# Two-layer decoder trunk in fp32: where transposes stand among matmuls, a diagonal level in 64-key parts, and the order of two row requests

## The reference

```
h    = rms_norm(x);  proj = h @ w_in               # q, f, i, gate of a gated recurrence, q, k, v of attention
y_hg = chunked_gated_recurrence(...)               # 4 heads of 128, decay from a cumulative sum
y_at = dilated_attention(...)                      # 8 heads of 64, three patterns merged
x    = x + concat(y_hg, y_at) @ w_out
q    = rms_norm(x) @ wq;  k, v = split(rms_norm(mem) @ wkv)     # 4 heads of 256, 256 memory tokens
x    = x + softmax(q k^T / 16) v @ wo
x    = x + moe(rms_norm(x))                        # 4 groups of 4 experts of width 512; best group, best 2 in it
```

## Time and profile before

| what | value |
|---|---|
| median of 3 runs | 1014.53 us (1013.32 to 1015.21) |
| profiled execution, its own time | 1015.3 us |
| its span, first to last instruction | 1013.4 us |
| TensorE busy | 988.4 us, 98% of the span |
| VectorE, ScalarE, GpSimd busy | 485.1, 136.5, 98.4 us |
| chain that ended last, by engine | PE 94%, DMA 2%, DVE 2%, POOL 1%, issue 1% |
| DMA, slices of 25.3 us from 811 to 988 us | 403, 421, 420, 420, 421, 420, 417 GB/s |
| mean granted TensorE clock | 0.993 of full speed |

### The profile page before, as it was taken

The page is one execution under the profiler, slowest core; times in us unless marked ns, Lnnn a source line. Parts: engine busy times, 40 slices in busy tenths (PEclk is TensorE's granted clock), DMA queues, the critical chain, the costliest instruction groups (busy, mean ns, idle before and its releaser), DMA issues.

```text
span 1013.4 us, 11694 instructions
## 1 busy us (share of the span) xinstructions
PE 988.4 (98%) x4744; PEld 532.2 (53%) x4744; DVE 485.1 (48%) x845; ACT 136.5 (13%) x323; POOL 98.4 (10%) x123
## 2 busy tenths in 40 slices
PE   8999999999998999999999999999999899999996
PEld 7658445669574453333333854465974333333332
DVE  2534386766554224422444636776656434444334
ACT  3211001412011010101112000041020101111111
POOL 3051032000020000000000513210000100000000
PEclk9999999999999999999999999999999999999999
DMA  9973101864289999999999420077385899999995
GB/s 356 425 310 122 45 1 48 372 249 163 88 309 377 397 424 419 420 423 420 421 422 420 180 84 1 1 288 284 133 316 210 340 403 421 420 420 421 420 417 200
DMA packets 44828, 293.61 MB, mean 290 GB/s; under 512 B 5472, under 2 KB 5728, under 8 KB 13024
## 3 DMA queue, kind: packets, MB, share of 16 engines
q1 hardware_dynamic: 38000, 266.36, 64.9%
q10 hardware_dynamic: 5616, 22.24, 5.6%
q0 software_dynamic: 1152, 4.19, 1.1%
HBM read 283.33 MB, written 9.44 MB: 289 GB/s over the span
## 4 chain that ended last, share of the span: by engine, by line
PE 94%; DMA 2%; DVE 2%; POOL 1%; issue 1%; ACT 0%; POOLq 0%; DVEq 0%; ACTq 0%
PE bank L1040 20%; PE bank L1110 11%; PE bank L598 8%; PE bank L1071 6%; PE bank L628 6%; PE bank L813 6%; PE bank L630 5%; PE bank L608 5%; PE bank L867 5%; PE bank L931 5%; PE bank L701 5%; PE bank L588 2%; DMA rot<-by_slot 2%; PE bank L901 1%; PE bank L885 1%; PE bank L1064 1%
## 5 line engine op out<-in xcount | busy, mean ns | idle before, releaser
L1040 PE MATMUL bank<-ring,hT 128*64 128x512 f32 x704 | 195.0, 593 | 0.0
L1040 PEld LDWEIGHTS bank<-ring,hT 128*64 128x64 f32 x704 | 62.3, 137 | 87.4 <-issue 87.4
L598 PE MATMUL bank<-ring,hT 128*128 128x512 f32 x192 | 85.6, 599 | 0.0
L1993 DVE TENSOR_TENSOR x<-bank,x 128x512 f32<-128x512 f32 x64 | 44.3, 692 | 51.1 <-PE bank L1071 51.1
L2011 DVE TENSOR_SCALAR xs<-xs 128x512 f32<-128x512 f32 x8 | 3.4, 427 | 124.2 <-ACT xs L1347 124.1
L1071 PE MATMUL bank<-PT 128*128 128x512 f32 x128 | 59.2, 605 | 0.0
L1110 PE MATMUL bank<-ring,Vx 128*64 128x512 f32 x160 | 57.9, 603 | 0.0
L598 PEld LDWEIGHTS bank<-ring,hT 128*128 128x128 f32 x192 | 35.5, 190 | 40.7 <-issue 40.2
L1110 PE MATMUL bank<-ring,xs 128*64 128x512 f32 x224 | 56.7, 595 | 0.0
L608 PE MATMUL bank<-hT,ring 128*128 128x256 f32 x256 | 55.7, 379 | 0.8 <-DVE hT L1622 0.8
L813 PE MATMUL bank<-ring,hT 128*128 128x512 f32 x128 | 56.3, 595 | 0.1
(11 more groups left out here) (302 smaller groups left out, 1550.0 us busy)
## 6 DMA issues: line engine op xcount, KB each, us to landing
ring<-in_w_experts SPq DMA_DIRECT2D x146, 1024.0 KB, 14.0
ring<-in_w_mix SPq DMA_DIRECT2D x60, 1024.0 KB, 14.1
work<-in_w_experts SPq DMA_DIRECT2D x20, 1024.0 KB, 11.2
late<-in_w_experts SPq DMA_DIRECT2D x10, 1024.0 KB, 13.2
late<-in_w_mix ACTq DMA_DIRECT2D x4, 2048.0 KB, 10.2
keys<-in_w_experts SPq DMA_DIRECT2D x8, 1024.0 KB, 16.4
rot<-by_slot ACTq DMA_DIRECT2D x14, 512.0 KB, 8.0
by_slot<-late ACTq DMA_DIRECT2D x1, 4096.0 KB, 37.9
```

Of the source, the lines that this page charges most:

```text
L598: last = nc.tensor.matmul(b[:, :], lhs[:, c, m * P:(m + 1) * P], w[:, c, :], start=(c == 0), stop=(c == C - 1))
L1040: last = nc.tensor.matmul(banks[2 + g][b2 * CAP:(b2 + 1) * CAP, :], rows_T_of(p)[:, c, b2 * CAP:(b2 + 1) * CAP], w, start=(c == 0), stop=( ...
L1993: V.tensor_tensor(xv, banks[OUT_BANK[n][m]][:, :], xv, ALU.add).then_inc(r_added[L], 1)
```

## The change

Four edits. (1) In both layers the transposes pt00 and pt01 go ahead of the scores sx11, on TensorE and in the order of banks; the vector engine's two copies go ahead of its maximum of sx11. By the bank plan sx11, pt00 and pt01 exchange the banks 4, 5 and 6. (2) In the first layer the eighth key-value job is cut: chunks 0 to 4, t1_00, t1_01, chunk 5, t1_10, chunks 6 and 7, t1_11. The second layer's order is as it was. (3) Level 0 is made in two 64-key parts like the levels above it, with 64 streamed, and copied in two parts. (4) In step p = 0 of the routed experts ScalarE waits for the scatter and requests the rows of pair 1 right after the first half of the gate unit, ahead of the read of the whole gate unit and of the exponential; the rows of pair 2 are requested after the exponential as before.

```diff
-             ("q_4", "A"), ("sx10", "A"), ("sx11", "A")]
-    jobs += [(f"pt0{jb}", "D") for jb in range(2)] + [("px0", "D"), ("px1", "A")]
+             ("q_4", "A"), ("sx10", "A")]
+    jobs += [(f"pt0{jb}", "D") for jb in range(2)] + [("sx11", "A"), ("px0", "D"), ("px1", "A")]
...
-                    for j in range(8):
+                    for j in range(7):
...
                     if L:
                         kv_job(7, banks[0], kv_unit, memT, chunks)
+                    else:
+                        kv_job(7, banks[7], unit("v1"), hT, chunks)
...
                         transposes(L, f"t1_{m}{c2}", by_columns(xs, m, c2))
-                    last_values(range(5, 6) if m == 0 else range(6, C))
+                        if (m, c2) == (0, 1):
+                            last_values(range(5, 6))
+                        elif (m, c2) == (1, 1 if L else 0):
+                            last_values(range(6, C))
...
-                                if j:
-                                    last = nc.tensor.matmul(b[HALF * i:HALF * (i + 1), a * QUARTER:(a + 1) * QUARTER], K[:, a, m * P + HALF * i:m * P + HALF * (i + 1)],
-                                                            later(Q[:, a, m * P + HALF * i:m * P + HALF * (i + 1)], j), start=True, stop=True)
-                            if j == 0:
-                                last = nc.tensor.matmul(b[:, a * P:(a + 1) * P], K[:, a, m * P:(m + 1) * P],
-                                                        Q[:, a, m * P:(m + 1) * P], start=True, stop=True)
+                                own = slice(m * P + HALF * i, m * P + HALF * (i + 1))
+                                n = QUARTER if j else HALF
+                                last = nc.tensor.matmul(b[HALF * i:HALF * (i + 1), a * n:(a + 1) * n], K[:, a, own],
+                                                        later(Q[:, a, own], j) if j else Q[:, a, own], start=True, stop=True)
...
                 memory_scores(1, 0, "q_2")
+                memory_weights(0)
                 memory_scores(1, 1, "q_4")
-                memory_weights(0)
...
                     if p == 0:
                         units_read(p, "half")
+                        act.wait_ge(r_sent[L], 16 * 2 * M)
+                        load_rows(1)
                     units_read(p, "gate")
-                    if p == 0:
-                        act.wait_ge(r_sent[L], 16 * 2 * M)
                     nc.scalar.activation(rexp_of[L], banks[2][:, :], ACT.Exp, scale=-1.0).then_inc(r_gexp[L], 1)
                     if p == 0:
-                        for q in (1, 2):
-                            load_rows(q)
+                        load_rows(2)
...
-                            emptied(V.copy_predicated(S[:, m, :, :], lev[:, j, :].bitcast(I32).unsqueeze(1).to_broadcast([P, HG_HEADS, P]),
-                                                      found[:, :].rearrange("p (a t) -> p a t", t=P)))
+                            for i in range(2):
+                                own = slice(HALF * i, HALF * (i + 1))
+                                copied = V.copy_predicated(S[own, m, :, own], lev[own, 0, own].bitcast(I32).unsqueeze(1).to_broadcast([HALF, HG_HEADS, HALF]),
+                                                           found[own, 0:HG_HEADS * HALF].rearrange("p (a t) -> p a t", t=HALF))
+                            emptied(copied)
...
                 memory_max(1, 0)
+                memory_kept(0)
                 memory_max(1, 1)
-                memory_kept(0)
```

## The result

| | before | after |
|---|---|---|
| median | 1014.08 us, 4 runs (1013.32 to 1015.21) | 1004.91 us, 4 runs (1003.76 to 1005.29) |
| profiled execution, span | 1015.3, 1013.4 us | 1003.76, 1001.8 us |
| TensorE busy | 988.4 us | 982.9 us |

The ratio of the runs is 0.9903, 95% interval 0.9888 to 0.9919: 9.8 us less, between 8.2 and 11.4 (the two medians alone differ by 9.2). A second series on another chip gave 1005.25 us (4 runs) and 0.9891 (0.9876 to 0.9906). The forecast was 1006.9, its range 1005.2 to 1009.6: the sign was right and the gain larger than forecast. Lines of the kernel after are 2 to 6 higher than before: L1064 became L1067, L1089 L1092, L1110 L1113, L1040 L1043, L885 L888, L901 L904, L701 L706, L739 and L736 both L742. "Landing" is the time from a DMA request to the arrival of its data.

The account below looks back on a forecast made before the run. TensorE, busy nearly the whole span, was taken as the bound. Terms 2.60 + 0.77 + 1.26 + 2.55 + 0.40 = 7.58 us off the profiled 1015.3 gave 1007.7, or 1006.9 against the median; range 1005.2 to 1009.6.

Parts of the forecast that it names:

- second layer's rows: Second layer's row stage: the earlier request lets rows land up to 0.8 us earlier with effect; gain taken 0.40 us.
- first layer's rows: First layer's row stage: request near 310.6, rows land before TensorE needs them, so the whole wait goes; gain 2.55 us.
- diagonal level: Level 0 in 64-key parts: 1.15 us instead of 1.78, 0.63 per layer, 1.26 us in all.
- Shares' transposes: Memory stage: the wait before the values goes, 1.30 us per layer, 2.60 us in all.
- rival (b): Memory stage: last shares come so late that their transposes wait, taking back 2.60 us: 1009.5 us; chance 0.08.
- Tokens: First layer's last key-value job: token transposes placed inside it remove the next projection's wait; gain 0.77 us.
- rival (e): Diagonal level takes 1.95 us, nothing of a piece hidden; 1.6 us back, 1008.5 us; chance 0.02.
- rival (a): First layer's row request queues behind the keys' load on ScalarE; 1.42 us of wait stays, 1008.3 us; chance 0.10.
- Rival (d), the clock: Second layer's row stage: half clock lasts on into the matmuls, making the kernel slower, up to 1026.7 us; chance 0.04.
- Rival (c), the weights: Second layer's weights run dry before the last down product; TensorE stalls 2.2 us, 1009.1 us; chance 0.07.

Follow-up runs that it names:

- the fillers: Kernel before plus two idle matmuls in the row stage of both layers, the first only, or the second only: ratios 0.9956, 0.9978, 0.9977.
- after_again: The changed kernel, unaltered, measured again beside a version with the second layer's old order of row requests: 1005.25 us, ratio 0.9891.
- the variants: Changed kernel with two idle matmuls in the second layer's row stage, its exponential ahead of the row request, or both: 1004.94, 1004.73, 1005.31 us.

## Where the prediction was right, and where it was wrong

The change is worth 7.58 us in the prediction's sum and 9.47 in the chains. Of the 1.89 between them 1.54 are in one term, the second layer's rows; 0.53 and 0.22 are the matmuls behind the waits that went, 0.07 the first layer's rows, and the diagonal level (0.24) and the end (0.23) go the other way. The median lies only 0.3 below the range, and the kernel before alone had medians from 1014.08 to 1015.98 on the chips used, but the gain is above the forecast's in both series.

- **Shares' transposes: right, too small.** The wait went and nothing took its place, so rival (b) is out; the spare time before the last transposes was 0.55, for 0.8 in the prediction. The upper bound was the wait, 1.30; measured 1.56 and 1.57. The first matmuls behind a wait had cost 0.27 more than the same ones in a running stream. The same at the tokens, 0.23.
- **Tokens: right**, 0.76 of wait, plus that 0.23.
- **Diagonal level: right.** 1.08 against my 1.15 and the 1.95 of rival (e); 0.19 came back in the job behind it, which I had not in the sum. By the rule of the Trainium skill, TensorE: Matmul & The Clock Gate, section Part 3, the prediction's estimate would have been the 1.95; these records, whose weights use all 128 rows, ran at 34 ns each, so the measurement decides against it. The vector engine's pair of 64x256 copies takes 0.89 to 0.90, the lower end of the 0.9 to 1.5.
- **First layer's rows: right**, 2.62 for 2.55. The wait went wholly, since the request left at 306.6 and took 8.4; rival (a) would have had it land behind 318.1, it was 315.0, with the keys' load in the same queue.
- **Second layer's rows: the step that failed.** "I take a gain of 0.4", with rows that land "up to 0.8 earlier with effect". The term took the 7.87 as fixed within a microsecond and let "fewer weights are ahead of the rows" count for under one microsecond. In fact the earlier 2 MB had been requested 6.8 before, the next stood 0.4 behind, and 7.87 became 4.4. With it the second of TensorE's two idle stretches went (2.30 and 1.14 before, 2.81 after, in the timelines of TensorE). That is 0.63 less idle time for the 0.4 of the sum. The other 1.31 of the 1.94 is the same work done faster, and the sum has no term for it: the clock was low for less long, and the down product of pair 0 alone has 7.10 instead of 8.23. That this hangs on the order is shown by the stage in eleven profiles (24.5 to 24.9 against 25.6 to 27.0); over the runs it is about 1 by the medians, not clear of nothing.
- **Rival (d), the clock: the right place with the wrong sign.** The wait for the activation did grow, to 2.8 for the forecast 2.7, and the clock did fall behind it (798 to 802 had 0.58), but for some 3.4 us (0.42 of 4 us, twice) instead of 6.8 (the earlier trace rows and its neighbours: 0.06, 0.50 and 0.29 of 4 us, twice). The prediction took only the last of the three, 1.2 us, for what was paid before. I asked what more idle time could cost and never what the idle time of before was costing: by the fillers about 4 us in all. The share of it that edit 4 brings back is in no term of the sum. Edit 4 alone took 4.6 us off with 4.35 in its chains (22.76 for 25.38, 24.89 for 26.62). Edit 1 took 4.4 with 3.1 in its chains; whether it touches the clock isn't shown.
- **Rival (c), the weights: near.** No matmul waited for weights, but the slack went from 1.1 to 0.3, the same kernel's last product took 7.25 in after_again, and the variants show the bound right behind it.

## What to carry to other kernels

A wait of TensorE is worth its length, a quarter of a microsecond for the matmuls behind it, and, behind the waits of 2.3 to 2.8 us here, what the clock loses in a part of the executions, which one profile may not show. Idle matmuls in the wait measure it, over many runs. A small urgent transfer that competes with large ones of another queue was quick here when they were issued behind it, even by 0.4 us, and the ones before were through. When a kernel is near two bounds, work out how much slack the other one has before summing gains: here the weights' stream took what three further variants gained in the row stage.

## What the runs showed of the hardware that was not expected

- A request of gathered rows took 3.8 to 4.9 us with 2 MB of another engine's requests 0.4 behind it and the 2 MB before 6.7 or more ahead, and 7.6 to 8.3 with 2 MB requested 3.0 to 3.5 ahead of it, or with 1 MB 0.07 ahead and 1 MB 0.31 behind.
- The granted clock fell behind the same 2.5 us wait in two of six profiles, and in the router stage in five of sixteen with no edit near it (14.6 to 15.2 us for work that took 14.1 in the others).
- Splitting a 128x128 fp32 product by keys into two halves, with twice the records, took 1.08 us instead of 1.78, though both forms stream 2048 columns in all (32 by 64, 16 by 128). The two halves write to different halves of the partitions; whether that is why was not tried.
- The first key job started between 10.40 and 12.38 us in the profiles, with the same code ahead of it: up to 2 us in a comparison of two single profiles here can be chance.
